# A sixth input chunk as seven products, the half token sums moved into the values' norms, and the pooled sums in a row

## The reference, cut to what matters

```python
h = x * (1.0 + sc[:, None]) + sh[:, None]
...
z = h @ w_in
a, ga, u, v, gb = jnp.split(z, [POOL_WIDTH, 2 * POOL_WIDTH, 2 * POOL_WIDTH + SGU_WIDTH,
                                2 * POOL_WIDTH + 2 * SGU_WIDTH], axis=-1)
ya = _multiscale_pool(a, pool_w, pool_scale) * jax.nn.silu(ga)
yb = _chunk_sgu(u, v, sgu_w, sgu_b) * jax.nn.silu(gb)
return jnp.concatenate([ya, yb], axis=-1) @ w_out
```

## Time and profile before

| | us |
|---|---|
| median of 3 runs | 2495.57 |
| lowest and highest | 2494.78, 2495.72 |
| the profiled execution | 2495.48 |
| its span, first to last instruction | 2493.4 |
| PE busy | 2467.5 (99%) |
| DVE busy | 1678.9 (67%) |
| ACT busy | 1182.7 (47%) |
| POOL busy | 125.0 (5%) |

### The profile page before, as it was taken

One profiled execution on the slowest core, in us unless ns is written; L12 is line 12 of the kernel. 1 busy time (PEld: TensorE's weight loads), 2 busy tenths in 40 slices (PEclk: granted clock), 3 DMA queues, 4 the chain that ended last, 5 costly groups with the idle time before them and its releaser, 6 DMA issues.

```text
span 2493.4 us, 41565 instructions
## 1 busy us (share of the span) xinstructions
PE 2467.5 (99%) x17056; PEld 2180.8 (87%) x17056; DVE 1678.9 (67%) x2839; ACT 1182.7 (47%) x2013; POOL 125.0 (5%) x177
## 2 busy tenths in 40 slices
PE   9999999999999999999999999999999999999999
PEld 7888887678999888877999988999888887899987
DVE  3787664667998444577799735899444477699833
ACT  4243435643555234576455433555333477455522
POOL 0240010001000000001000000000000001000000
PEclk9999999999999999999999999999999999999999
DMA  7625141112333223222333332333333221333321
GB/s 310 243 104 177 35 115 38 35 60 85 102 102 115 89 85 107 71 67 69 103 117 102 108 113 68 119 102 108 113 102 99 65 65 62 100 102 103 119 101 68
DMA packets 182731, 252.29 MB, mean 101 GB/s; under 512 B 13073, under 2 KB 156689, under 8 KB 178193
## 3 DMA queue, kind: packets, MB, share of 16 engines
q1 hardware_dynamic: 182544, 249.65, 30.6%
HBM read 247.53 MB, written 2.10 MB: 100 GB/s over the span
## 4 chain that ended last, share of the span: by engine, by line
PE 91%; DVE 4%; ACT 2%; issue 1%; POOL 1%; DMA 1%; DVEq 0%; SPq 0%; POOLq 0%; ACTq 0%
PE psum L909 88%; PE psum L1580 1%; PE psum L1463 1%; PE psum L981 1%; PE psum L1682 0%; ACT w_hi L1757 0%; DVE stats_first L2507 0%; DVE work L2500 0%; POOL stats_first L3406 0%; DVE X L2503 0%; DMA u_gated<-in_l_cd_w_mod 0%; DVE w_lo L2399 0%; ACT work L1812 0%; POOL stats_mix L3406 0%; DVE w_lo L2726 0%
## 5 line engine op out<-in xcount | busy, mean ns | idle before, releaser
L909 PE MATMUL psum<-h_hi,w_hi 128*128 128x256 f32 (+1 forms) x1392 | 446.1, 320 | 1.2 <-DVE w_lo L2399 1.2
L909 PE MATMUL psum<-h_hi,w_lo 128*128 128x256 f32 (+1 forms) x1392 | 440.4, 316 | 0.0
L909 PE MATMUL psum<-h_lo,w_hi 128*128 128x256 f32 (+1 forms) x1392 | 440.2, 316 | 0.0
L2399 DVE TENSOR_TENSOR w_lo<-raw,w_hi 128x2048 fp32r<-128x2048 f32 (+2 forms) x94 | 211.8, 2258 | 267.6 <-ACT w_hi L1757 267.0
L1757 ACT ACTIVATE w_hi<-raw 128x2048 fp32r<-128x2048 f32 (+2 forms) x95 | 178.7, 1886 | 261.2 <-PE psum L909 251.4
L909 PEld LDWEIGHTS psum<-h_hi,w_hi 128*128 128x128 f32 x1392 | 265.3, 191 | 23.6 <-issue 5.3
L909 PEld LDWEIGHTS psum<-h_hi,w_lo 128*128 128x128 f32 x1392 | 265.3, 191 | 17.6
L909 PEld LDWEIGHTS psum<-h_lo,w_hi 128*128 128x128 f32 x1392 | 265.5, 191 | 15.6 <-issue 0.2
L909 PE MATMUL psum<-w_hi,ff_hi 128*128 128x512 f32 x576 | 224.9, 390 | 1.2 <-DVE ff_lo L3187 1.2
L909 PE MATMUL psum<-w_lo,ff_hi 128*128 128x512 f32 x576 | 224.1, 389 | 0.0
L909 PE MATMUL psum<-w_hi,ff_lo 128*128 128x512 f32 x576 | 224.1, 389 | 0.0
(11 more groups left out here) (443 smaller groups left out, 5410.8 us busy)
## 6 DMA issues: line engine op xcount, KB each, us to landing
raw<-in_ffn_w_gate SPq DMA_DIRECT2D x44, 1024.0 KB, 5.4
raw<-in_ffn_w_up SPq DMA_DIRECT2D x44, 1024.0 KB, 5.4
raw<-in_ffn_w_down SPq DMA_DIRECT2D x44, 1024.0 KB, 4.9
raw<-in_w_in SPq DMA_DIRECT2D x36, 512.0 KB, 5.0
raw<-in_l_ab_w_in SPq DMA_DIRECT2D x10, 1024.0 KB, 7.9
mod_w<-in_l_ab_w_mod SPq DMA_DIRECT2D x8, 1024.0 KB, 18.3
raw<-in_w_out SPq DMA_DIRECT2D x8, 1024.0 KB, 5.0
u_gated<-in_l_cd_w_mod SPq DMA_DIRECT2D x6, 1024.0 KB, 6.2
```

The costliest lines, as they stand in the source:

```text
L909: return pe.matmul(o, lhsT, rhs, start=start, stop=stop, skip_group_check=True)
L2399: dve.tensor_tensor(lo[:, 0:nk * n], raw[c % 2][:, 0:nk * n], hi[:, 0:nk * n].bitcast(F32), ALU.subtract).then_inc(*w_lo_made.mark(key))
```

## The change

**Chunk 2 joins the fast chunks.** `AB_FAST` becomes (2, 3, 8, 9, 4, 5), and chunk 2's four `group` steps go. The first products' weights (`first_parts`) and the rests of the tokens of products 5 and 7 now follow the rest of product 6 inside chunk 1, and the rest of product 4 follows chunk 1. The two split buffers change places for the mixed weights. The gate products 20 to 23 go with the first two fast chunks. `ab_target` puts chunk 2 in `silu_ga` beside chunk 3.

**Six half sums move.** A new function `plain_half` makes half of one of the four sums of high part and rest. `v_norms` calls it for each of the six tiles, between the variance and the wait for POOL's power; `mix_tokens` makes the last two.

**Two tables of counts.** The tables of groups 1 and 3 go to a second buffer, `u_gated[:, 3, :]`. A table is loaded when the group two before it is done. The block of chunk 9 that is written there waits for the last group.

```diff
-AB_FAST = (3, 8, 9, 4, 5)
+AB_FAST = (2, 3, 8, 9, 4, 5)
...
+AB_BEHIND = {(0, 0): [("turned", 14, 15)], (0, 1): [("mod", 16, 17)], (1, 0): [("turned", 16, 17), ("rounded",), ("first_parts", 0)], (1, 1): [("mod", 18, 19)]}
...
+        if _q < 2:
+            _n = 20 + 2 * _q + _part
+            AB_STEPS += [("turned", *((18, 19) if _n == 20 else (_n - 1,))), ("mod", _n)]
...
-                sp.wait_ge(*(pooled[g - 1] if g else psum_full["modp", 8 + 11]))
-                sp.dma_start(inv_cnt[:, :], A["k_inv_count"][g].partition_broadcast(P)).then_inc(*count_landed.mark(g))
+                sp.wait_ge(*(pooled[g - 2] if g > 1 else psum_full["modp", 7 if g else 8 + 11]))
+                sp.dma_start(counts_of[g], A["k_inv_count"][g].partition_broadcast(P)).then_inc(*count_landed[g % 2].mark(g))
...
+            inv_count(1)
+            inv_count(0)
+            late(12)
             raws_to(6)
-            inv_count(0)
-            for m in range(12, 15):
-                late(m)
+            late(13)
+            inv_count(2)
+            late(14)
+            inv_count(3)
             raws_to(7)
             late(15)
...
-                act.wait_ge(*(psum_full["fast", "ab", q - 1, 5] if q else psum_full["used", ("ab_in", 1)]))
+                act.wait_ge(*(psum_full["fast", "ab", q - 1, 5] if q else psum_full["used", ("ab_in", 7)]))
...
+            def plain_half(n):
+
+                dst, (hi, lo) = ((ab_t_plain[5][0], ab_block(0, 1)), (by_k(x_plain, 0), ab_block(0, 0)), (ab_t_plain[7][0], ab_block(1, 1)),
+                                 (by_k(ab_stage, 0), ab_block(1, 0)))[n // 2]
+                at = slice(2 * (n % 2), 2 * (n % 2) + 2)
...
+                dve.tensor_tensor(dst[:, at, :], hi[:, at, :].bitcast(F32), lo[:, at, :].bitcast(F32), ALU.add).then_inc(*fast_t.mark(("ab", "plain")))
...
                 bias_variance(("v", t), v_stat(t, 7), 1.0)
+                plain_half(t)
                 dve.wait_ge(*rsqrt_made["v", t])
...
             def middle_blocks(q):
...
+                if AB_FAST[q] == 9:
+                    dve.wait_ge(*pooled[3])
...
                 elif kind == "first_parts":
                     first_parts(0)
                     first_rests(0)
+                    tokens_rest(5)
+                    tokens_rest(7)
```

More of the change, by code:

```diff
@@ L86 @@
 AB_STEPS += [("end", 7), ("mix",)]
[L87 to L95, removed]
+AB_BEHIND = {(0, 0): [("turned", 14, 15)], (0, 1): [("mod", 16, 17)], (1, 0): [("turned", 16, 17), ("rounded",), ("first_parts", 0)], (1, 1): [("mod", 18, 19)]}
+for _j in range(2):
+    for _r in range(2):
+        AB_STEPS += [("group", 1, _j, _r), *AB_BEHIND[_j, _r]]
+AB_STEPS += [("end", 1), ("last_rounded",)]
 for _q in range(len(AB_FAST)):
@@ L161, in add @@
         plan.append(what)
-    for ch in (6, 0, 7, 1, 2, *AB_FAST):
+    for ch in (6, 0, 7, 1, *AB_FAST):
         add(("ab_in", ch), "ab_w_in", 0, "cols", ch * CW, CW, True)
@@ L290, in build @@
         pre_g_landed = signal("pre_g_landed", 16)
-        count_landed, post_g_landed = signal("inv_count_landed", 16), signal("post_g_landed", 16)
+        count_landed, post_g_landed = [signal(f"inv_count_landed_{i}", 16) for i in range(2)], signal("post_g_landed", 16)
         g_row_landed, b_row_landed = signal("g_row_landed", 16), signal("b_row_landed", 16)
@@ L431, in build @@
         sgu_b = sb(ab, "sgu_b", [P, 4, P])
+        counts_of = [u_gated[:, 3, :] if g % 2 else inv_cnt[:, :] for g in range(4)]
         late_w = [t[:, 0:3, :].rearrange("p a b -> p (a b)")[:, 0:KT * CW].rearrange("p (k n) -> p k n", n=CW) for t in (u_gated, silu_ga)]
@@ L589, in ab_target @@
             ch = AB_FAST[q]
-            tile, g = silu_ga if ch == 3 else u_gated, 2 * (ch % 2)
+            tile, g = silu_ga if ch < 4 else u_gated, 2 * (ch % 2)
             return tile[:, g:g + 2, :].rearrange("p a b -> p (a b)")
@@ L2654, in mix_tokens @@
                 b11, b21 = by_k(x_plain, 0), by_k(ab_stage, 0)
-                dve.wait_ge(*scaled_act["xs", 3, 0])
-                dve.wait_ge(*scaled_act["xc", 3])
-                dve.wait_ge(*part_made["sum", ("xs", 3, 1)])
-                dve.wait_ge(*h_lo_made["xc", 3])
-                for dst, b in ((t1, ab_block(0, 1)), (b11, ab_block(0, 0)), (t3, ab_block(1, 1)), (b21, ab_block(1, 0))):
-                    m = dve.tensor_tensor(dst, b[0].bitcast(F32), b[1].bitcast(F32), ALU.add)
-                m.then_inc(*fast_t.mark(("ab", "plain")))
+                plain_half(6)
+                plain_half(7)
                 dve.wait_ge(*fast_t["ab", "plain"])
@@ L3428, in gpsimd_program @@
                     o, a = PAD_OFF[r] - window // 2, pooled_in[:, g, PAD_OFF[r]:PAD_OFF[r] + n]
-                    pool.tensor_tensor(src[:, o:o + n], src[:, o:o + n], inv_cnt[:, off:off + n], ALU.mult).then_inc(*pooled.mark(("mean", g, r)))
+                    pool.tensor_tensor(src[:, o:o + n], src[:, o:o + n], counts_of[g][:, off:off + n], ALU.mult).then_inc(*pooled.mark(("mean", g, r)))
                     pool.wait_ge(*pooled["mean", g, r])
```

46 lines of the change are left out of this document (22 added, 24 removed).

## The result

| | before | after |
|---|---|---|
| median of 7 runs, us | 2496.07 | 2503.97 |
| ratio, 95% interval | | 1.0033 (1.0023 to 1.0043) |
| profiled execution, us | 2495.48 | 2504.38 |
| its span, us | 2493.4 | 2502.3 |

The changed kernel is slower by 0.33%, 7.9 us between the medians. The forecast was 2503.1 with a range of 2498 to 2508.5, and it named "slower" with 75%.

What follows compares the result with a forecast made beforehand. TensorE, 91% of the span, was taken as the bound, with VectorE feeding it: 13.6 us of new gaps, less 3.7 of old ones and 2.3 of columns, gave +7.6, 2503.1 us, range 2498 to 2508.5.

Steps and rivals of the forecast that it cites:

- Columns: Chunk 2 as seven products takes PE 14.5 us where a plain chunk without gate products takes 16.8: 2.3 saved.
- Half sums: Six sums moved into the norm waits delay each tile 0.63 us, but PE waits for none: cost 0, gain 0.
- First weight rest: At the first seven-product chunk, due at 108.1, PE waits 2.0 us for DVE's weight rest, ready at 110.0.
- Stage copy behind product 4's rest: Before product 2 of the first chunk, PE, through at 114.2, waits 3.9 us for ACT's copy, ending at 118.1.
- Rest of S3 and S4 in the first chunk: DVE's weight rest, slowed by POOL, is ready at 125.5; PE, through with product 5 at 123.6, waits 1.9 us.
- gate weights 21: Weights queued behind a raw chunk arrive at 134.3, PE is there at 132.0: it waits 2.3 us.
- third chunk: The second weight rest comes at 158.8 behind POOL's four widest sums; PE wants it at 157.5: 1.3 us.
- Second chunk: The rest comes at 145.0, gate weights at 153.8, PE at 151.6: PE waits 2.2 us for the weights.
- Rival C: PE runs slow behind the new 3.9 us gap, losing 2.8 more: +10.4 us, 2505.9; chance 18%.
- POOL's hold of DVE: Pooled-sum instructions hold DVE 1.4, 0.9 or 0.5 us each by width, 25 us in all.
- In a row: Pooled sums run from 112.9 to about 160, so all 25 us of holds fall on three chunks with 13 free.
- Rival B: Only the front chain counts: 5.9 us of new waits against 6.0 saved, 2495.4, no change; chance 15%.

Runs made afterwards that it cites:

- run 1: Kernel before with only the six half token sums moved into VectorE's waits for the values' norms: 1.0000 of the kernel before.
- run 2: Changed kernel with GpSimd's window sums and means left out, an 8-column product per group in their place: 0.9993 of the kernel before, median 2494.76 us.
- run 7: Changed kernel with VectorE's token rest of product 4 put ahead of that of product 7: 1.0029 of the kernel before.
- run 6: Changed kernel with gate weights 21 and 23 issued ahead of the raw chunk they stood behind in SP's queue: 1.0029 of the kernel before.
- Run 3: Changed kernel with the pooled sums spaced as before, one table of counts, six fast chunks and half sums kept: 1.0025 of the kernel before.
- run 4: Kernel before with only the pooled sums put in a row, two tables of counts, five fast chunks: 1.0004 of the kernel before.
- run 9: Changed kernel, GpSimd's 26 pooled instructions paced by chunks' last weight rests, product 4's token rest ahead of product 7's: 1.0013 of the kernel before, median 2499.3 us.
- run 10: As run 9, with the first chunk's weights also made before the last plain chunk ends: 1.0008 of the kernel before, median 2498.7 us.
- run 12: As run 10, with GpSimd's fourth group split over three chunks and gate weights 21 ahead of the raw chunk: 0.9994 of the kernel before, median 2495.02 us.
- run 8: Changed kernel with GpSimd's row of pooled sums begun only after the first chunk's last weight rest: 1.0026 of the kernel before, median 2503.0 us.

## Why the prediction was right

- **Columns, -2.3.** The sum as written doesn't give it: 84 matmuls at 13.00 / 76 are 14.4, not 14.5, and with 16.8 that saves 2.4. But a chunk of seven products without gate work takes 14.6 in the changed kernel (DVE's step L2737 starts at 165.68, 180.28 and 194.87), and half a plain chunk is 10.44 - 2.00 = 8.44, a chunk 16.9: 16.9 - 14.6 is 2.3. No run changes the columns alone; the balance of +7.1 against a measured 7.0 leaves little room for another value.
- **Half sums, 0.** Right: 1.65 to 1.77 a power, ending 0.9 after the sum, no wait of PE, 1.0000 in run 1. The mixing ended at 102.1 (102.2 forecast).
- **First weight rest, 2.0.** 2.03, for the reason given (ACT's high half, done at 108.3).
- **Stage copy behind product 4's rest, 3.9.** 3.46. In run 2 it is 2.15, so POOL's part is 1.3.
- **Rest of S3 and S4 in the first chunk, 1.9; gate weights 21, 2.3; third chunk, 1.3.** These three terms were mis-sized: 0, 0.52 and 0 were measured, 5.0 us too much together. The rests came about as forecast (124.55 for 125.5; 157.96 for 158.8; gate weights at 133.2 for 134.3). What was wrong is PE's side: I let it arrive at full pace (121.1 by the measured start), and it came at half, 123.9. In run 7, with PE held by only 0.48 and not slowed ahead of it, the wait for that rest is 3.94.
- **Second chunk.** 0.59 for the rest, which I had at 0, and 2.04 for gate 23, which I had at 2.2.
- **Rival C, half pace behind the long gap, +2.8.** It happened, and once more, 1.7, behind the gap of 2.04, though behind as long a gap at 107.7 the clock kept 1.00. That the first cost 2.8, as forecast, is luck: behind the same gap run 6 lost 1.7. I priced it as an addition to the gaps. It stood in their place: 4.5 of pace for 5.0 of waits. That the sum came out at 13.1 for 13.6 is not two errors cancelling by luck: with other gaps and another pace, the stage was 107.3 long in run 6 and 107.2 in run 7, for 107.4, and both are bounded by the same rests of DVE. What is luck is the last step, to the whole time: the stage cost 7.0 for a forecast 7.6, and the 1.0 at the end of the program, for which there was no term, brought it to the measured 7.9.
- **The range.** Its upper edge doesn't follow from the terms it names: rival C with the early POOL step is 7.6 + 2.8 + 1.8, 2507.7; only with the 0.7 of tile 3's bank is it 2508.4.
- **POOL's hold of DVE, 25 us.** 20.9 by run 2. The bound I gave (20) was nearer than the value. Without this work the six chunks give 0.9993, with it 1.0033. But the forecast took the 3.5 of waits that the kernel before paid for it as saved, so by the estimate of run 2 about half of the loss is the new front's.
- **"In a row" as the cause.** Here the prediction said too much. I argued that before the groups fell on four chunks and now on three. Run 3 puts them on four again and gains nothing that the times can tell, and run 4 puts them in a row with five fast chunks and loses nothing; the traces put the row at 1.5 to 1.7 of the 7.0. The greater cause is the sixth seven-product chunk, which takes away the plain chunk behind which the first operands were made and beside which POOL's first group cost PE nothing. That DVE has no such place left fits all runs, but no run shows it alone. Of the runs that keep both the sixth chunk and the sums, only the paced ones (9, 10, 12) gave time back.
- **Rival B** (only the front counts, 2495.4) was wrong for the changed kernel but gives run 2 almost exactly, 2494.8. In part that is luck: of its gaps, the 1.4 for gate weights was not there, and 1.6 of half pace was.

What stays open: which gaps are followed by half pace; what the 1.0 at the end of the program is; what the window sums cost the kernel before; and how much of run 12's 8 us is the pacing and how much the early first weights, as they were not run apart (run 10 against run 9 can't be told from no change).

## What to carry to other kernels

When two engines take turns and one of them feeds the bound engine, a gap or a slow stretch of the bound engine is worth nothing until the feeder's next result comes earlier: find the result whose time stays put when the gap is closed (here the third chunk's second weight rest, at 158 in the changed kernel and in runs 6, 7 and 8). Before a sparse piece of work is replaced by a denser one, ask what used to run beside it for nothing. And here a helper engine's work did better when paced by the feeder's own events, in small lots with the wide instructions apart, than laid in a row (run 8 moved that row as a block and gained nothing). When a piece of work is taken out to price it, take it out of both kernels.

## What the runs showed of the hardware

- In the changed kernel PE worked at half pace for 5.7 us behind a gap of 3.46 (2.8 lost) and for 3.4 us behind 2.04 (1.7 lost). Behind 1.76 and 0.49 in run 4 it came too, behind 3.43 in run 6 it cost 1.7, and behind 2.73 it came in run 9 and not in run 10: the length of the gap just ahead does not decide alone. It differs between executions of one kernel, too: the mean granted clock over the span was 1.000 in the two shortest executions of run 10 (2496.42 and 2496.81) and 0.998 in the two longest (2500.38 and 2501.09).
- A DVE instruction of two inputs beside POOL's: a 791-wide sum held product 4's rest 1.3 us (3.06 in the changed kernel, 1.75 in run 2), and 26 instructions of POOL held DVE 20.9 us in all, 0.8 each (against run 2, where 8 of 8 columns stand in their place).
- A power of 4 columns behind a 768-wide sum of DVE took 1.65 to 1.77 for 1.03, all six times and again in run 1.
- A 128-column matmul of the constant leaves two records and takes 0.22 us at full clock.
